# The sample tile's projections in two passes over a paired stationary of 64 columns

## The reference, cut to what matters

```python
h = rms_norm(x, lp['g_mix'])
z = h @ lp['w_in']
rq, rk, rv, rg, dq, dk, dv, ga, gb = jnp.split(z, SPLIT_IDX, axis=-1)
rq = rope(rq.reshape(B, T, RET_HEADS, RET_DK), pos)            # retention: 4 heads, 128 / 128 / 256 columns
rk = rope(rk.reshape(B, T, RET_HEADS, RET_DK), pos) * (RET_DK ** -0.5)
dq = rope(rms_norm(dq.reshape(B, T, DA_HEADS, 2, DA_DK), lp['g_qn']), pos)   # differential attention
dk = rope(rms_norm(dk.reshape(B, T, DA_HEADS, 2, DA_DK), lp['g_kn']), pos)   # 4 heads, 2 maps of 128 each
dv = dv.reshape(B, T, DA_HEADS, DA_DV)                         # 256 columns
```

## Time and profile before

| | before |
|---|---|
| time, median of 3 runs | 2243.19 us (2242.13 to 2244.16) |
| the profiled execution's own time | 2242.92 us |
| its span in the profile | 2241.1 us |
| TensorE busy | 2222.3 us, 99% of the span |
| VectorE, ScalarE, GpSimd busy | 1078.2, 654.7, 666.0 us |
| mean granted clock of TensorE | 0.999 of full speed |

### The profile page before, as it was taken

The page is one execution under the profiler, slowest core; times in us unless marked ns, Lnnn a source line. Parts: engine busy times, 40 slices in busy tenths (PEclk is TensorE's granted clock), DMA queues, the critical chain, the costliest instruction groups (busy, mean ns, idle before and its releaser), DMA issues.

```text
span 2241.1 us, 34167 instructions
## 1 busy us (share of the span) xinstructions
PE 2222.3 (99%) x13160; PEld 2091.9 (93%) x13160; DVE 1078.2 (48%) x2032; ACT 654.7 (29%) x1519; POOL 666.0 (30%) x368
## 2 busy tenths in 40 slices
PE   8999999999999999999999999999999999999999
PEld 7999777789898898998999999999999999999999
DVE  5312444445535455355145658666666663313432
ACT  5200333335535345354212222110101104334311
POOL 4522210230130400401350534223333325576520
PEclk9999999999999999999999999999999999999999
DMA  7622222230130310302851322222222126656311
GB/s 253 198 92 76 71 69 88 76 103 27 32 108 27 105 40 25 118 27 72 301 169 61 116 64 76 76 67 70 72 66 76 57 68 202 187 162 203 97 50 49
DMA packets 312666, 218.18 MB, mean 97 GB/s; under 512 B 16330, under 2 KB 303677, under 8 KB 312542
## 3 DMA queue, kind: packets, MB, share of 16 engines
q1 hardware_dynamic: 219802, 117.33, 18.1%
q10 hardware_dynamic: 92740, 99.15, 13.1%
HBM read 160.15 MB, written 56.29 MB: 97 GB/s over the span
## 4 chain that ended last, share of the span: by engine, by line
PE 94%; ACT 3%; DMA 1%; issue 1%; DVE 1%; ACTq 1%; DVEq 0%
PE ps L606 28%; PE ps L608 28%; PE ps L607 27%; PE ps L830 3%; PE ps L857 2%; PE ps L780 1%; PE ps L785 1%; PE ps L995 1%; PE ps L782 1%; PE ps L848 1%; ACT L1426 1%; ACT L1377 1%; DMA scr<-inv_d 0%; ACT full L1370 0%; PE ps L833 0%
## 5 line engine op out<-in xcount | busy, mean ns | idle before, releaser
L606 PE MATMUL ps<-a_hi,w_hi 128*128 128x352 f32 x2928 | 950.1, 324 | 5.3 <-DVE a_lo L1674 3.2
L608 PE MATMUL ps<-a_hi,w_lo 128*128 128x352 f32 x2928 | 940.3, 321 | 0.0
L607 PE MATMUL ps<-a_lo,w_hi 128*128 128x352 f32 x2928 | 939.5, 321 | 0.0
L504 POOL TENSOR_SCALAR w_hi<-w_raw 128x1024 fp32r<-128x1024 f32 x150 | 162.9, 1086 | 1435.8 <-PE ps L608 877.5
L606 PEld LDWEIGHTS ps<-a_hi,w_hi 128*128 128x128 f32 x2928 | 549.6, 188 | 9.3 <-issue 8.6
L607 PEld LDWEIGHTS ps<-a_lo,w_hi 128*128 128x128 f32 x2928 | 550.9, 188 | 0.4
L608 PEld LDWEIGHTS ps<-a_hi,w_lo 128*128 128x128 f32 x2928 | 550.4, 188 | 0.0
L506 POOL TENSOR_TENSOR w_lo<-w_raw,w_hi 128x1024 fp32r<-128x1024 f32 x150 | 363.5, 2423 | 12.5
L606 PE MATMUL ps<-w_hi,a_hi 128*128 128x384 f32 (+3 forms) x864 | 318.7, 369 | 0.0
L608 PE MATMUL ps<-w_hi,a_lo 128*128 128x384 f32 (+3 forms) x864 | 307.7, 356 | 0.0
L607 PE MATMUL ps<-w_lo,a_hi 128*128 128x384 f32 (+3 forms) x864 | 306.5, 355 | 0.0
(11 more groups left out here) (206 smaller groups left out, 2283.4 us busy)
## 6 DMA issues: line engine op xcount, KB each, us to landing
w_raw<-w_in SPq DMA_DIRECT2D x64, 512.0 KB, 4.2
w_raw<-w_down SPq DMA_DIRECT2D x48, 512.0 KB, 3.6
w_raw<-w_up SPq DMA_DIRECT2D x44, 512.0 KB, 3.7
hid_d<-scr ACTq DMA_DIRECT2D x22, 512.0 KB, 2.6
w_raw<-w_down SPq DMA_DIRECT2D x24, 384.0 KB, 3.2
scr<-gates_d ACTq DMA_DIRECT2D x24, 352.0 KB, 6.1
gates_d<-full ACTq DMA_DIRECT2D x13, 528.0 KB, 2.6
xt_d<-full ACTq DMA_DIRECT2D x1, 4224.0 KB
```

Of the source, the lines that this page charges most:

```text
L504: pool.tensor_scalar(hi, raw, 1.0, 0.0, ALU.mult, ALU.add).then_inc(S["w_hi_done"], 1)
L606: pe.matmul(out, lhs[0], rhs[0], start=start, stop=False)
L607: pe.matmul(out, lhs[0], rhs[1], start=False, stop=False)
L608: return pe.matmul(out, lhs[1], rhs[0], start=False, stop=stop)
```

## The change: two passes with both halves side by side

For the sample tile alone, `a_hi` and `a_lo` of its 32 tokens are put side by side as one stationary of 64 columns (`pairs`, eight blocks `[hi | lo]`, copied once by ScalarE ahead of the retention). `project` then makes two matmuls for each `k` instead of three, one with `w_hi` and one with `w_lo`. Rows 0 to 31 of the bank receive the part of `a_hi`, rows 32 to 63 that of `a_lo` (with the product low x low, which was left out before). The halves have to be added: ScalarE copies the upper rows from PSUM to SBUF (`folded`, `folded2`), and VectorE adds them to the lower rows in PSUM. In retention ScalarE does the copy and waits for the add ahead of its value copy. In the attention the nine early matmuls of the sample tile go behind the transposes; in the step after, ScalarE's copy takes the place of the four squares, and the squares follow after the add, behind the first root. Some buffers move to make room (half of the mask, `q_d`).

```diff
+        pair_at = ((full_at + 4 * f.at, 3), (scr_at + 4 * s.at, 2), (u_last_at + 4 * 12 * 4, 2),
+                   (full_at + 4 * (mask_at + P), 1))
+        pairs = [sample_pair(f"pair{j}", at, n) for j, (at, n) in enumerate(pair_at)]
+        def folded(n):
+            return rope_b[0:NS, 0:n]
+        def folded2():
+            return scr[0:NS, 0:2 * 3 * P].rearrange("p (b n) -> p b n", b=2)
+        def fold_count(h, diff):
+            return TILES + len(pairs) * 2 + HEADS * diff + h + 1
...
# TensorE
             def project(bank, i, s0, s1, k0=0, k1=KT):
                 r, n = rows(i), (s1 - s0) * P
+                if i == LAST:
+                    out = ps[0:2 * r, bank, 0:n].rearrange("p (s c) -> p s c", c=P)
+                    for k in range(k0, k1):
+                        pe.matmul(out, pair(k), w_hi[:, s0:s1, k * P:(k + 1) * P], start=k == 0, stop=False)
+                        last = pe.matmul(out, pair(k), w_lo[:, s0:s1, k * P:(k + 1) * P], start=False, stop=k == KT - 1)
+                    return last
...
-                    project(2 * (i % 2), i, PA_SLOT, PA_SLOT + 3, k1=EARLY)
+                    if i < LAST:
+                        project(2 * (i % 2), i, PA_SLOT, PA_SLOT + 3, k1=EARLY)
...
-                    project(2 * (i % 2), i, PA_SLOT, PA_SLOT + 3, k0=EARLY).then_inc(S["pa_done"], 1)
+                    project(2 * (i % 2), i, PA_SLOT, PA_SLOT + 3, k0=EARLY if i < LAST else 0).then_inc(S["pa_done"], 1)
...
# ScalarE, ahead of the retention
+            act.wait_ge(S["lo_done"], TILES)
+            for j, k0 in enumerate(pair_k0):
+                n = pair_at[j][1]
+                for m, part in enumerate((a_hi_k, a_lo_k)):
+                    act.activation(pairs[j][:, :, m, :], part[:, k0:k0 + n, NP:NT].bitcast(F32), ACT.Copy).then_inc(S["x_ev"], 1)
...
# ScalarE, retention, ahead of the value copy
+                    if i == LAST:
+                        act.wait_ge(S["rope_done"], 2 * n)
+                        act.copy(folded(4 * P), ps[NS:2 * NS, n % 3, 0:4 * P]).then_inc(S["x_ev"], 1)
+                        act.wait_ge(S["diag_done"], TILES + n // TILES + 1)
...
# ScalarE, attention, where the four squares stood (they are head_squares now)
+                    if i == LAST:
+                        act.wait_ge(S["pb_done"], n + 1)
+                        act.wait_ge(S["d_tr"], n - 1)
+                        act.copy(folded2(), ps[NS:2 * NS, 0:2, 0:3 * P]).then_inc(S["x_ev"], 1)
+                    else:
+                        head_squares(n)
...
                 if turned:
+                    if i == LAST:
+                        act.wait_ge(S["diag_done"], TILES + HEADS + h + 1)
+                        head_squares(n)
                     act.wait_ge(S["d_sq"], 4 * (n + 1))
...
# VectorE, retention, ahead of the rotation
+                    if i == LAST:
+                        dve.wait_ge(S["x_ev"], fold_count(h, 0))
+                        dve.tensor_tensor(ps[0:NS, n % 3, 0:4 * P], ps[0:NS, n % 3, 0:4 * P], folded(4 * P),
+                                          ALU.add).then_inc(S["diag_done"], 1)
...
# VectorE, attention, behind the copy of the transposed weights
+                if turned and turned[1] == LAST:
+                    h = turned[0]
+                    dve.wait_ge(S["x_ev"], fold_count(h, 1))
+                    dve.tensor_tensor(ps[0:NS, 0:2, 0:3 * P], ps[0:NS, 0:2, 0:3 * P], folded2(),
+                                      ALU.add).then_inc(S["diag_done"], 1)
```

More of the change, by code:

```diff
@@ L129, in kernel_program @@
         a_pre = nc.alloc_sbuf_tensor_at("a_pre", [P, KT * NT], F32, offset=a_lo_at)
+        full_at = -(-nc.sbuf_base // 32) * 32
         full = sb("full", [P, KT * NT])
+        scr_at = -(-nc.sbuf_base // 32) * 32
         scr = sb("scr", [P, 6 * UW])
@@ L136, in kernel_program @@
         convs = sb("convs", [P, 2, 2 * FT])
+        u_last_at = -(-nc.sbuf_base // 32) * 32
         u_last = sb("u_last", [P, 2 * FT, 4])
@@ L234, in kernel_program @@
         gqk = f.take(2 * P).rearrange("p (g c) -> p g c", g=2)
+        mask_at = f.at
         mask = f.take(2 * P)
@@ L251, in kernel_program, with sample_pair, pair @@
         st = s.take(48)
+        def sample_pair(name, at, n):
+            return nc.alloc_sbuf_tensor_at(name, [P, n, 2, NS], F32R, offset=at)
+        pair_at = ((full_at + 4 * f.at, 3), (scr_at + 4 * s.at, 2), (u_last_at + 4 * 12 * 4, 2),
+                   (full_at + 4 * (mask_at + P), 1))
+        assert f.at + 3 * 2 * NS <= KT * NT and s.at + 2 * 2 * NS <= 6 * UW
+        pairs = [sample_pair(f"pair{j}", at, n) for j, (at, n) in enumerate(pair_at)]
+        pair_k0 = (0, 3, 5, 7)
+        def pair(k):
+            j = max(j for j in range(4) if pair_k0[j] <= k)
+            return pairs[j][:, k - pair_k0[j], :, :].rearrange("p m n -> p (m n)")
+        def folded(n):
[4 more added lines that the diff above has]
+            return TILES + len(pairs) * 2 + HEADS * diff + h + 1
         at = nrm_at + 256
@@ L261, in kernel_program @@
         qk_t = full[:, k_t_at + 640:k_t_at + 1152].rearrange("p (b n) -> p b n", b=2)
-        q_d = full[:, at + NT + HC:at + NT + HC + 2 * P].rearrange("p (b n) -> p b n", b=2)
+        q_d = (full[:, k_t_at + 1152 + NT:k_t_at + 1152 + NT + P],
+               scr[:, e1_at + 2 * NT + HC:e1_at + 2 * NT + HC + P])
         gate_row = gates_h[0][0]
@@ L739, in _ @@
                         pe.wait_ge(S["gate_ev"], n + 1)
+                    if n == LAST:
+                        pe.wait_ge(S["x_ev"], TILES + len(pairs) * 2)
                     project(n % 3, i, 4 * (h % 2), 4 * (h % 2) + 4).then_inc(S["ret_proj"], 1)
@@ L781, in _ @@
                     if i:
-                        last = pe.matmul(out, q_d[:, n % 2, 0:r], (s_p if i < LAST else s_s)[h % 2],
+                        last = pe.matmul(out, q_d[n % 2][:, 0:r], (s_p if i < LAST else s_s)[h % 2],
                                          start=False, stop=True)
@@ L1220, in _ @@
             act.wait_ge(S["g_scaled"], 1)
-            act.dma_start(mask[0:1, :], t["c_mask"]).then_inc(S["head_const"], 16)
+            act.dma_start(mask[0:1, 0:P], t["c_mask"][:, 0:P]).then_inc(S["head_const"], 16)
+            act.dma_start(mask[0:1, P + P // 2:2 * P], t["c_mask"][:, P + P // 2:2 * P]).then_inc(S["head_const"], 16)
+            act.wait_ge(S["lo_done"], TILES)
[3 more added lines that the diff above has]
+                    act.activation(pairs[j][:, :, m, :], part[:, k0:k0 + n, NP:NT].bitcast(F32), ACT.Copy).then_inc(S["x_ev"], 1)
             def head_loads(h):
@@ L1338, in chunk_sigmoid, with head_squares @@
                 act.activation(chunk(q), chunk(q), ACT.Sigmoid).then_inc(S["gate_sig"], 1)
+            def head_squares(n):
+                r, b = rows(n % TILES), n % TILES % 2
+                for m in range(4):
+                    if m == 3:
+                        act.wait_ge(S["pb_done"], n + 1)
+                    bank, at = (2 * b, m * P) if m < 3 else (2 * b + 1, 0)
+                    act.activation(nrm[0:r, m * P:(m + 1) * P], ps[0:r, bank, at:at + P], ACT.Square,
+                                   accum_out=st[0:r, 8 + 4 * b + m:9 + 4 * b + m]).then_inc(S["d_sq"], 1)
             for s in range(DIFF_STEPS):
@@ L1365, in _ @@
                         act.wait_ge(part_st[1], h * 48)
[L1366 to L1369, removed]
-                        act.activation(nrm[0:r, m * P:(m + 1) * P], ps[0:r, bank, at:at + P], ACT.Square,
-                                       accum_out=st[0:r, 8 + 4 * b + m:9 + 4 * b + m]).then_inc(S["d_sq"], 1)
+                    if i == LAST:
+                        act.wait_ge(S["pb_done"], n + 1)
+                        act.wait_ge(S["d_tr"], n - 1)
+                        act.copy(folded2(), ps[NS:2 * NS, 0:2, 0:3 * P]).then_inc(S["x_ev"], 1)
+                    else:
+                        head_squares(n)
                 if normed:
```

4 lines of the change are left out of this document (2 added, 2 removed).

## The result

| | before | after |
|---|---|---|
| time, median | 2243.45 us (4 runs, 2242.13 to 2244.16) | 2255.01 us (4 runs, 2252.34 to 2255.11) |
| ratio to before | | 1.0047, 95% interval 1.0035 to 1.0059 |
| the profiled execution, its span | 2242.92, 2241.1 us | 2255.11, 2253.3 us |

What follows compares the result with a forecast made beforehand. TensorE, busy 99% of the span, was taken as the bound. Attention's four times +3.5 us (+14.0) less retention's 7.4 us gave +6.6 us on 2242.92 us: 2249.5, stated as 2249.8 us; range 2243.5 to 2258 us.

Steps and rivals of the forecast that it cites:

- Retention: Sample tile's retention projections: two passes instead of three save 1.84 us a head, 7.4 us for four, all counted.
- The step of the projection: Attention, sample tile projected: first half's 1.39 us becomes waiting, second scores start as now; second half gives its 1.39 us.
- The step after: Attention, sample tile normalised: ScalarE's queue waits for VectorE's add; second scores come 3.5 us later a head.
- One link: Attention, step after: line 1399 releases the value product at 600.7, 2.0 us later than now, after 3.4 us idle.
- The sum: Whole kernel: attention's +14.0 us less retention's 7.4 us is +6.6 us, giving 2249.8 us; the forecast's chance was 0.61.
- a sign that it would be wrong: Profile after: the granted clock falling behind the long wait, listed beside waits under 1 us and retention gaining under 5 us.
- the upper end: Range's top, 2258 us: a clock that falls in all heads and a little dearer chain.
- rival 1: Attention: the long wait also slows TensorE's clock, 1.7 us a head, 6.8 us more, 2256.6 us; chance 0.17.
- Rival 2: Retention and attention: chains finish early, TensorE keeps all 18.5 us of saved matmuls, 2224.7 us; chance 0.07.
- rival 3: Attention, step after: line 1399 late by 2.0 us but not the exponential; 8.0 less 7.4 us, 2243.8 us; chance 0.15.

Runs made afterwards that it cites:

- experiment 1: Kernel before with only retention taking the two passes over 64 columns, attention as before: 2234.67 us, ratio 0.9959.
- experiment 5: Changed kernel with six of the 16 matmuls of the sample tile's first half put ahead of the first scores again: 2256.15 us, ratio 1.0051.
- experiment 3: Changed kernel with ScalarE's normalised output (former line 1399) moved ahead of its wait for the add: 2255.48 us, ratio 1.0048.
- experiment 6: Changed kernel with ScalarE's normalised output and two scaled copies of the stored output moved ahead of its wait for the add: 2254.15 us, ratio 1.0041.
- experiment 4: Changed kernel with 24 gate matmuls a head made twice in the place of the long wait, same result: 2250.09 us, ratio 1.0028.
- experiment 7: Kernel of experiment 6 with the value product of the step after the sample tile made three times, same result: 2246.32 us, ratio 1.0005.
- experiment 8: Changed kernel with the attention's copy and add moved into the tail of the projecting step, squares back in their old place: 2232.85 us, ratio 0.9951.
- experiment 2: Changed kernel with VectorE's attention add moved to the head of its step, ahead of reciprocal and reduction: 2235.19 us, ratio 0.9960.
- experiment 9: Changed kernel with the edits of experiment 5 and experiment 8 together: 2233.76 us, ratio 0.9953.

## Why the prediction was right, and where its size was off

**Retention** was right. The sample tile's projections of heads 0 and 1 start 66.55 us apart; before it was 68.43 (252.20 to 320.63). That is 1.88 us a head, 7.5 in all, where 7.4 was forecast, and experiment 1 finds nothing given back. The order in time around the fold (to be read against the earlier trace rows):

```profile
252.75 0.47 PE L750 MATMUL ps<-w_hi,pair 128*64 128x512 f32 x1
...
319.30 0.48 PE L750 MATMUL ps<-w_hi,pair 128*64 128x512 f32 x1
```

```profile
256.70 0.58 ACT L1307 COPY scr<-ps 32x512 f32<-32x512 f32 x1 [1.95 <-PE ps L751]
258.04 0.47 ACT L1311 ACTIVATE full<-ps,u_last 32x256 f32<-32x256 f32 x1 [0.76 <-DVE ps L1863]
```

Counted from the projection's first matmul, the value copy starts 5.29 us later, before it was 5.81 (252.20 to 258.01): 0.5 us sooner, where the working gave 0.4. The copy and the add take 0.58 and 0.69 us, where 0.65 was taken for each.

**The step of the projection** was right. The wait for VectorE's copies is 0.40 us (0.45 forecast). Set against the kernel before, the second scores of that step come only 0.28 us sooner in head 0 and not at all in the other three: the first half's 1.39 us is lost, as experiment 5 shows from the other side. The second half gives 1.35 us. TensorE's wait for the exponential there is 0.62 us, where the prediction looked for 1 us or more.

**The step after** was right along ScalarE's chain. Counted from its first scores (585.63), the add starts 4.15 us later (4.15 forecast) and takes 0.94 us (0.97), line 1464 starts at 7.33 us (7.38), and the exponential ends with its read-out at 11.32 us (11.4). One link was wrong without changing the sum: the value product started at 8.47 us and not at 7.9, since it waits for the scaled copies too (experiments 3 and 6). The exponential behind them decides, and it stood in the chain already. With that later start the 1.3 us of waiting for the exponential that the prediction looked for shrink to 0.61 us while the clock is kept (experiment 4), and to nothing where the value product runs slowly.

**The clock is the term that was mis-sized.** The sum had none. The prediction had named a granted clock that falls behind the long wait as a sign that it would be wrong, and that sign showed; that the time still lies in its range is because the upper end left room for this. The clock was put aside as rival 1, for which the prediction allowed 0.17, because TensorE had done transposes alone before the idle time of the earlier trace rows, and dense products before the new one. That reason was wrong: after 3.84 us of idle behind dense gate matmuls the clock fell in all four heads. TensorE's distance to the kernel before can be read at two places, the attention's first scores and the last transposes of an output; here they are for the kernel before, the changed kernel and experiment 4:

```profile
503.39 0.38 PE L830 MATMUL ps<-full,scr 128*128 128x128 f32 x2
...
1076.25 0.31 PE L1011 MATMUL ps<-ident,scr 32*128 32x32 f32 x2
```

```profile
496.44 0.38 PE L871 MATMUL ps<-full,scr 128*128 128x128 f32 x2
...
1087.78 0.31 PE L1053 MATMUL ps<-ident,scr 32*128 32x32 f32 x2
```

```profile
497.57 0.38 PE L871 MATMUL ps<-full,scr 128*128 128x128 f32 x2
...
1084.88 0.31 PE L1054 MATMUL ps<-ident,scr 32*128 32x32 f32 x2
```

Between them it grows by 18.5 us in the changed kernel and by 14.5 us with work in the wait; 14.0 was forecast. So the clock cost 4.0 us in that profiled run, about 1.0 us a head: some 0.7 to 0.8 us in three heads, 1.7 us in head 2, whose stretch shows 0.50 throughout. Rival 1 had 1.7 us a head. It is less where the slow value product takes the place of a wait: in experiment 4 TensorE idles 0.61 us ahead of the second scores of that step, in the changed kernel it does not. Where nothing stood between the wait and the path, in experiment 6, the second scores took 1.8 us more in head 0. Of the 5.6 us by which that run misses the sum (its span is 12.2 us longer, 6.6 were forecast) 4.5 lie between the two places, 0.4 ahead of them and 0.7 behind; for these last two no run here names a cause, but single runs of one kernel differ by more (last section).

The Trainium skill, page "TensorE: Matmul & The Clock Gate", section "Why this matters for your kernels", says that an idle gap between bursts of matmuls puts the clock back to half rate. The runs agree: behind waits of 3.2 to 3.8 us it fell, and with the same waits filled (experiments 4 and 7) it stayed at 1.00. By that rule the time was rival 1's, 2256.6 us, and the measured 2255.0 us is nearer to it than to the forecast.

Rival 2 (all matmuls count, 2224.7 us) and rival 3 (the exponential not late, 2243.8 us) were both ruled out by the change as it stands: the add stood where the prediction put it, and the exponential ended 0.1 us from the forecast. Of rival 2's 18.5 us the best order, experiment 8, reaches 10.9 by the medians.

## What to carry to other kernels

When an operation is added to a chain, look at what stands ahead of it in the engine's own queue: the add cost 0.94 us, and its place behind a reduction that waits for the next step's products cost some 5 us a head, the clock included (2255.0 against 2235.2 us in experiment 2). Work taken off the busiest engine pays only where no other chain ends at the same point, so order the new small operations into the tail of the step that makes their input. Price an idle gap on TensorE of the length seen here (3.2 to 3.8 us) at the gap and the slow clock behind it, ask what stands directly behind the gap, and do not count on the clock behind one of some 2 us either (next section).

## What the runs showed of the hardware that was not expected

- The clock fell late in every wait of 3.2 to 3.8 us or just behind it, though TensorE had been full of matmuls before: sixteen waits, four each in the changed kernel and in experiments 3, 5 and 6. Stretches behind waits of 0.4 to 0.6 us showed 1.00.
- Behind the attention every one of these kernels has one more wait, in which TensorE, full of matmuls up to it, idles 1.9 to 2.3 us for VectorE. The clock fell there in seven of the eleven profiled runs (the changed kernel and experiments 1, 2, 3, 5, 6, 7) and stayed at 1.00 in the kernel before and in experiments 4, 8 and 9. From the end of this wait to the end of the span it is 1143.8 to 1144.8 us where it fell and 1142.2 to 1143.2 us where it did not. So single runs of one kernel can differ by some 1.5 us by this alone, and of the 4.9 us between experiment 4 and the changed kernel a part may be this wait's; how much is not shown. The stretches behind the wait, in the kernel before (2.09 us of waiting, up to 1097.91) and in the changed kernel (2.12 us, up to 1109.48):

```profile
1098.00:1102.00 4.00, 4.00 (x25) 4.00 (x26) 1.92 (x5) 1.63 (x3) 0.00 (x0) 1.00 1.07 398
```

```profile
1109.00:1113.00 4.00, 3.52 (x15) 3.55 (x16) 2.49 (x6) 2.12 (x3) 0.00 (x0) 0.69 1.06 398
```

- The same fall had different prices: 0.7 to 1.7 us a head where the slow work ran in part beside another wait, 1.4 to 2.8 us where it was all on the path (experiment 6 against 7). Filling the gap with work that is thrown away made the kernel faster by 4.9 and by 7.8 us.
- A stationary of 64 columns costs a matmul over 384 columns the same as one of 32: 343 against 346 ns.
